# Two transformer blocks on one core: the feed-forwards in two phases, their down products by seven, each down unit passing four banks once per product kind

## The chip, the cores and the metric

The kernel runs on one core of one Trainium2 chip. The metric is the device time in microseconds, the median of several runs. Smaller is better.

## What is computed

Two transformer blocks in a row on a sequence of 1024 tokens of width 1024, in float32. The change touches only their two feed-forwards:

```python
def conv_glu(hn, w_up, conv_f_w, conv_f_b, w_down):          # first block
    up = hn @ w_up
    gate = jax.nn.gelu(causal_dwconv(up[..., :D_FF], conv_f_w, conv_f_b), approximate=False)
    return (gate * up[..., D_FF:]) @ w_down
...
    y = (jax.nn.silu(u @ w_gate[l]) * (u @ w_up[l])) @ w_down[l]   # second block
```

D_FF is 2816 and CONV_F is 3. The result of each is added to the running activations, in the second block after a norm.

## The kernel before

Activations lie transposed, channels on the 128 partitions and tokens along the row. A float32 product is made of three passes: weights and activations are each split into a high and a low part, and high x high, high x low and low x high are summed in PSUM. One matmul has 128x128 weights and 512 columns.

The 2816 hidden channels are 22 tiles, handled as 11 chunks of two tiles (FC = 11). The first chunk's gate and up products are made in the plain way. For each of the other ten, two *pairs* (a gate tile and an up tile each) are made by Strassen's scheme: seven products of 12 matmuls (`part_product`, L1104; four blocks of 128 channels, three passes each) in place of eight. Each product's result goes to a PSUM bank of its own (`pair_banks`), and VectorE combines them (`pair`, L2855), scales them by the norm, applies the convolution in the first feed-forward (`gate_in`), and multiplies gate and up (`hidden`, L2853). Between the pairs of one chunk and those of the next stands the down product of the chunk before (`down_half`, L1157): 8 output tiles x 2 hidden tiles x 2 halves x 3 passes, 96 matmuls, whose results VectorE adds to the running sum in `W` (`add_down`, L2909). The last chunk's down product stands at the end (`last_half`).

The weights come in parts of 128x512 (`part`, over `w_raw`), fetched by SyncE. For each part or sum of parts, ScalarE makes the high part (`high`, L1897) and POOL the low part (`low`, L559) into a ring of three places. POOL also makes the four sums of parts per pair that the scheme needs (L566, L571, L575, L577). VectorE makes the low parts of activations (`diff_lo`, L2798, `act_lo`) and of the hidden tiles (`g_lo`, L2899). Each engine has its own list of instructions in program order; semaphores tie them: `parts_high` and `parts_split` count high and low parts, `product_quarters` products of TensorE, `evacuated` the results that VectorE took away.

Per chunk TensorE has 2 x 84 + 96 = 264 matmuls. The loop over chunks is a hardware loop, whose first and last turn are written out.

```python
for k in range(4):
    w = slice(k * P, (k + 1) * P)
    for i, (a, x) in enumerate(((ring_hi, hi), (ring_hi, lo), (ring_lo, hi))):
        last = pe.matmul(out, a[slot][:, w], x(k), start=(k == 0 and i == 0), stop=(k == 3 and i == 2))
```

## Time and profile before

| | |
|---|---|
| median of 3 runs | 2813.38 us (2813.02 to 2814.61) |
| span of the profiled execution | 2812.4 us |
| TensorE busy | 2756.6 us, 13262 matmuls |
| VectorE busy | 1763.2 us |
| POOL busy | 1365.9 us |
| ScalarE busy | 1027.8 us |
| first feed-forward | about 719 to 1357 us |
| second feed-forward | about 2160 to 2790 us |

Busy time of TensorE is of pipelined matmuls whose durations overlap (one shows 0.389 us), so their pace is read from start to start or from the chain of work that ended last. PE is TensorE, DVE is VectorE, ACT is ScalarE, POOL is GpSimd and SP is SyncE. A line "L559" is a line of the kernel.

### The profile page before, as it was taken

The numbers are of one execution on the slowest core, as the hardware profiler recorded it, in microseconds if no ns is written. First come the engines' busy times: TensorE is split into PE (matmuls) and PEld (weight loads), VectorE is DVE, ScalarE is ACT, GpSimd is POOL, SyncE is SP. The second block draws the span as 40 slices with busy tenths as digits, with TensorE's granted clock in tenths as the row PEclk, the third lists the DMA queues.
The fourth block names the chain that finished last, engine by engine and source line by source line (L and its number), as shares of the span: only waits on it lengthen the run. The fifth ranks groups of instructions, "written<-read, shape, count | busy, mean of one in ns | idle before, by whom it ended". The sixth has DMA issues, their size and how long they took to land.

```text
span 2812.4 us, 36491 instructions
## 1 busy us (share of the span) xinstructions
PE 2756.6 (98%) x13262; PEld 2267.9 (81%) x13262; DVE 1763.2 (63%) x1889; ACT 1027.8 (37%) x1638; POOL 1365.9 (49%) x774
## 2 busy tenths in 40 slices
PE   8999999999999999999999999999999999999999
PEld 6888788888788888888887777778876888888886
DVE  7988552336976667776845446883369656555556
ACT  4256531332422222222413435553456222222224
POOL 4322212214666667666566331543254765566663
PEclk9999999999999999999999999999999999999999
DMA  4101322011111111112322110432023111111113
GB/s 151 38 23 38 105 97 83 31 67 46 46 52 45 52 52 48 63 52 82 128 92 96 46 38 17 140 114 82 23 96 118 49 56 60 48 47 55 51 56 134
DMA packets 72274, 191.31 MB, mean 68 GB/s; under 512 B 7792, under 2 KB 8048, under 8 KB 71408
## 3 DMA queue, kind: packets, MB, share of 16 engines
q1 hardware_dynamic: 61920, 157.12, 16.7%
q10 hardware_dynamic: 10256, 32.86, 3.2%
q8 instruction: 65, 1.06, 0.2%
q14 instruction: 33, 0.27, 0.0%
HBM read 172.65 MB, written 17.30 MB: 68 GB/s over the span
## 4 chain that ended last, share of the span: by engine, by line
PE 57%; issue 23%; POOL 12%; DVE 4%; ACT 2%; DMA 1%; POOLq 0%; ACTq 0%; DVEq 0%; SPq 0%
PE products L651 20%; PE products L1111 8%; PE others L1111 7%; PE others L1157 5%; PE products L1157 5%; POOL w_lo L559 4%; POOL w_lo L502 2%; POOL w_raw L577 1%; POOL w_raw L575 1%; PE others L651 1%; PE products L1047 1%; DVE work L2427 1%; DMA w_raw<-wstream 1%; POOL w_raw L566 1%; POOL part_sum L571 1%
## 5 line engine op out<-in xcount | busy, mean ns | idle before, releaser
L559 POOL TENSOR_TENSOR w_lo<-w_raw,w_hi 128x512 fp32r<-128x512 f32 x328 | 464.5, 1422 | 442.1 <-ACT w_hi L1897 441.1
L1897 ACT ACTIVATE w_hi<-w_raw 128x512 fp32r<-128x512 f32 x328 | 207.1, 633 | 815.9 <-PE products L1111 209.6
L499 POOL TENSOR_TENSOR w_hi<-w_raw,small 128x1024 fp32r<-128x1024 f32 x54 | 111.1, 2058 | 583.9 <-PE products L651 326.4
L651 PE MATMUL products<-act_hi,w_hi 128*128 128x512 f32 x864 | 346.9, 402 | 1.4 <-DVE act_lo L2383 1.3
L651 PE MATMUL products<-act_lo,w_hi 128*128 128x512 f32 x864 | 337.5, 391 | 0.0
L651 PE MATMUL products<-act_hi,w_lo 128*128 128x512 f32 x864 | 337.5, 391 | 0.0
L502 POOL TENSOR_TENSOR w_lo<-w_raw,w_hi 128x1024 fp32r<-128x1024 f32 x94 | 253.0, 2691 | 144.6 <-ACT w_hi L2226 140.4
L651 PEld LDWEIGHTS products<-act_hi,w_hi 128*128 128x128 f32 x864 | 162.9, 189 | 42.0 <-issue 7.3
L651 PEld LDWEIGHTS products<-act_hi,w_lo 128*128 128x128 f32 x864 | 162.7, 188 | 35.0
L651 PEld LDWEIGHTS products<-act_lo,w_hi 128*128 128x128 f32 x864 | 163.2, 189 | 31.4 <-issue 0.2
L745 PE MATMUL products<-act_hi,w_hi 128*128 128x512 f32 x408 | 167.0, 409 | 7.4 <-DVE act_lo L3329 4.7
L1111 PE MATMUL products<-diff_hi,w_hi 128*128 128x512 f32 x400 | 157.8, 395 | 9.6 <-POOL w_lo L559 5.9
L745 PE MATMUL products<-act_lo,w_hi 128*128 128x512 f32 x408 | 159.8, 392 | 0.0
L745 PE MATMUL products<-act_hi,w_lo 128*128 128x512 f32 x408 | 159.7, 391 | 0.0
L1111 PE MATMUL products<-diff_hi,w_lo 128*128 128x512 f32 x400 | 156.4, 391 | 0.0
L1111 PE MATMUL products<-diff_lo,w_hi 128*128 128x512 f32 x400 | 156.3, 391 | 0.0
L1111 PE MATMUL others<-act_hi,w_hi 128*128 128x512 f32 x400 | 155.6, 389 | 0.0
L1111 PE MATMUL others<-act_lo,w_hi 128*128 128x512 f32 x400 | 155.6, 389 | 0.0
L1111 PE MATMUL others<-act_hi,w_lo 128*128 128x512 f32 x400 | 155.6, 389 | 0.0
L2864 DVE TENSOR_TENSOR work<-work,products 128x512 f32<-128x512 f32 x40 | 27.5, 687 | 179.6 <-PE products L1111 175.8
L2909 DVE TENSOR_TENSOR work<-work,others 128x1024 f32<-128x1024 f32 x76 | 92.7, 1220 | 66.8 <-PE others L1157 64.7
L2909 DVE TENSOR_TENSOR work<-work,products 128x1024 f32<-128x1024 f32 x76 | 92.5, 1217 | 61.7 <-PE products L1157 61.7
(555 smaller groups left out, 6928.0 us busy)
## 6 DMA issues: line engine op xcount, KB each, us to landing
w_raw<-wstream SPq DMA_DIRECT2D x155, 512.0 KB, 3.3
w_raw<-wstream SPq DMA_DIRECT2D x248, 256.0 KB, 2.6
work<-xT ACTq DMA_DIRECT2D x16, 512.0 KB, 8.8
parked<-work ACTq DMA_DIRECT2D x8, 512.0 KB, 3.0
work<-parked ACTq DMA_DIRECT2D x8, 512.0 KB, 5.1
parked<-work ACTq DMA_DIRECT2D x2, 2048.0 KB, 8.7
work<-parked SPq DMA_DIRECT2D x8, 512.0 KB, 7.6
out<-work SPq DMA_DIRECT2D x16, 256.0 KB, 2.3
```

The costliest lines, as they stand in the source:

```text
L499: pool.tensor_tensor(w_hi[:, slot, :], w_raw[:, slot, :], zeros, ALU.add)\
L502: pool.tensor_tensor(w_lo[:, slot, :], w_raw[:, slot, :], w_hi[:, slot, :].bitcast(F32), ALU.subtract).then_inc(s("weights_split"), 1)
L559: pool.tensor_tensor(ring_lo[slot], source, ring_hi[slot].bitcast(F32), ALU.subtract).then_inc(s(signal), 1)
L566: pool.tensor_tensor(part[2], part[0], part[2], ALU.subtract).then_inc(s("parts_summed"), 1)
L571: pool.tensor_tensor(part_sum[:, :], part[3], part[2], ALU.subtract).then_inc(s("parts_summed"), 1)
L575: pool.tensor_tensor(part[0], part_sum[:, :], part[0], ALU.add).then_inc(s("parts_summed"), 1)
L651: last = pe.matmul(out[:, c], a[:, ws, w], x[:, k, c], start=(k == 0 and i == 0), stop=(k == KT - 1 and i == 2))
L745: last = pe.matmul(out, a[:, b % 2, w], x[:, k, c], start=(k == 0 and i == 0), stop=(k == KT - 1 and i == 2))
L1111: last = pe.matmul(out, a[slot][:, w], x(k), start=(k == 0 and i == 0), stop=(k == 3 and i == 2))
L1157: last = pe.matmul(out(2 * n + o)[0][:, t], a[slot][:, w], x(k)[:, t], start=(k == 0 and i == 0), stop=(k == 1 and i == 2))
L1897: act.activation(ring_hi[slot], source, ACT.Copy).then_inc(s("parts_high"), 1)
L2909: dve.tensor_tensor(W[:, o, :], W[:, o, :], down_slots[o % 4], ALU.add).then_inc(s("evacuated"), 1)
```

## The change

**Two phases.** The ten chunks' gate and up pairs now follow each other without a down product between them. Each finished hidden tile is stored in DRAM (`parked_hidden`). After the last pair comes the down product of the first ten chunks as a whole, made by Strassen's scheme as well: outputs, hidden channels and tokens are each halved. It is made in two rounds of five chunks (ROUNDS, ROUND). A round has seven steps (kinds 0 to 6 of products), a step five units, one for each chunk, and a unit 12 matmuls: four output tiles, each in a bank of its own, times three passes. 70 units have 840 matmuls where there were 960. The eleventh chunk's down product stays as it was.

**A unit** (`down_unit`) first passes the four banks with high x high, then with high x low after a wait for VectorE's low part, then with low x high after a wait for POOL's. Results of a chain of steps stay in PSUM (four banks for even steps, four for odd), and VectorE adds them to `W` once per step (`step_added`), 128x512 four times.

**The operands of a unit.** Weight tiles and hidden tiles of a round (20 of 512 KB) are loaded into places that the activations, their differences and their low parts leave (`down_upper`, `down_lower`, `hidden_first`, `hidden_second`), in the first round while the last pair still runs. For kinds 1 to 4 POOL makes one sum of weights per unit (`down_sum`) and VectorE one of hidden tiles (`factor_sum`). The high parts are both ScalarE's, the low of the weights is POOL's (`down_low`), that of the hidden tiles VectorE's (`factor_low`). There are four places for each, so that the high part of unit u waits for the end of unit u-4.

**The pairs** are made in another form of the scheme (Winograd's): sums of products are accumulated in PSUM in three banks per pair, and ScalarE copies a bank's intermediate value out three times (`copied`) before the next product goes on in it. VectorE combines four times per pair in place of seven. One of the low parts gets a fourth place. VectorE's operations of scaling and convolution of a pair are done at the start of the next one. The order of the low parts of differences at the start is another: in the second feed-forward those of the third difference come last, and TensorE's third product waits for eight low parts (four before), the fourth and fifth for twelve (eight and twelve).

Core of the diff:

```diff
-        part_sum = place("part_sum", [P, HALF], F32, over="w_hi", offset=HALF)
+        part_sum = place("part_sum", [P, HALF], F32, over="w_lo", offset=HALF)
+        down_hi, down_lo = ring_hi, ring_lo
+        ring_lo = [*ring_lo[0:3], g_hi[:, 0, 0:HALF]]
+        RING = (0, 1, 2, 0, 1, 2, 3)
...
-        part_source = [part[0], part[1], part[2], part_sum[:, :], part[0], part[1], part[3]]
+        part_source = [part[0], part[1], part_sum[:, :], part[0], part[2], part[1], part[3]]
...
+        parked_hidden = nc.dram_tensor("parked_hidden", (2 * BLOCKED, P, T), F32, kind="Internal").ap()
...
+                    sp.wait_ge(s("parts_split"), of.high(c, 7 * j + 6))
+                    fetch(1, at + gate)
+                    if first:
+                        store_hidden(0, 0)
+                    if j:
+                        store_hidden(c, 0)
+                    else:
+                        store_hidden(c + (-1), 1)
+                    sp.wait_ge(s("parts_split"), of.high(c, 7 * j + 7))
+                    fetch(3, at + up)
...
+                for product, first, second in ((2, (0, 1), ()), (3, (2, 3), ()), (4, (4,), (0, 1))):
+                    sp.wait_ge(s("product_quarters"), of.quarters(FC - 1, 8 + product))
+                    for i in first:
+                        down_tiles(i, 0)
+                        hidden_tiles(i, 0, 0)
+                    for i in second:
+                        hidden_tiles(i, 0, 1)
+                sp.wait_ge(s("product_quarters"), of.quarters(FC - 1, 8 + 6))
+                for i in (2, 3, 4):
+                    hidden_tiles(i, 0, 1)
+                down_tiles_lower(0, 0)
...
+                def down_sum(r, s_, i):
+
+                    n = sum_after(r, s_, i)
+                    if s_ == 1:
+                        pool.wait_ge(s("parts_split"), of.down_high(STEP_UNITS * r + i))
+                        k, count = tile_loaded(AT_FFN[name], "second", i, r)
+                        pool.wait_ge(s(f"x_in{k}"), count)
+                        ins = pool.tensor_tensor(a11(i), a11(i), a21(i), ALU.subtract)
+                    elif s_ == 2:
...
+                        ins = pool.tensor_tensor(spare_w(name, i), a22(i), a11(i), ALU.subtract)
+                    elif s_ == 3:
+                        ins = pool.tensor_tensor(a21(i), a21(i), a22(i), ALU.add)
+                    else:
+                        pool.wait_ge(s("parts_split"), of.down_high(STEP_UNITS * r + ROUND + i))
+                        pool.wait_ge(s("parts_summed"), of.down_summed(sum_after(r, 2, i)))
+                        ins = pool.tensor_tensor(a12(i), a12(i), spare_w(name, i), ALU.subtract)
+                    ins.then_inc(s("parts_summed"), 1)
+
+                def down_low(u):
+
+                    source, slot = part[u - UNITS] if u >= UNITS else down_source(name, *unit_of(u)[1:]), down_slot(u)
+                    pool.wait_ge(s("parts_high"), of.down_high(u))
+                    low_, high_ = (down_lo[slot], down_hi[slot]) if u >= UNITS else (by_o(down_lo[slot]), by_o(down_hi[slot]))
+                    pool.tensor_tensor(low_, source, high_.bitcast(F32), ALU.subtract).then_inc(s("parts_split"), 1)
+
+                chunk(1, True)
+                with pool.Fori(2, FC) as c:
+                    chunk(c)
+                for u in range(UNITS + 4):
+                    if u + 1 < UNITS and 1 <= unit_of(u + 1)[1] <= 4:
+                        down_sum(*unit_of(u + 1))
+                    down_low(u)
...
+                def pair(c, j, after_first=False):
+
+                    n = 7 * j
+                    chain_, other, alone = (bank(m) for m in pair_banks[j])
+                    if not after_first:
+                        pe.wait_ge(s("evacuated"), of.evacuated(c, 4 * j - 4))
+                    part_product(c, n + 1, chain_, *lower_half)
+                    if after_first:
+                        pe.wait_ge(s("evacuated"), of.first_evacuated + 2)
+                    part_product(c, n + 2, alone, *lower_second)
+                    pe.wait_ge(s("parts_copied"), of.copied(c, 3 * j + 1))
+                    part_product(c, n + 3, chain_, *difference[1], start=False)
+                    if after_first:
+                        pe.wait_ge(s("evacuated"), of.first_evacuated + 5)
+                    part_product(c, n + 4, other, *difference[0])
+                    pe.wait_ge(s("parts_copied"), of.copied(c, 3 * j + 2))
+                    part_product(c, n + 5, chain_, *third, start=False)
+                    pe.wait_ge(s("parts_copied"), of.copied(c, 3 * j + 3))
+                    part_product(c, n + 6, other, *upper_second, start=False)
+                    pe.wait_ge(s("evacuated"), of.evacuated(c, 4 * j + 2))
+                    part_product(c, n + 7, chain_, *upper_half, start=False, done=2)
+
+                def down_unit(u):
+
+                    r, s_, i = unit_of(u)
+                    g, slot, x = STEPS * r + s_, down_slot(u), u % 4
+                    pe.wait_ge(s("parts_high"), of.down_high(u))
+                    pe.wait_ge(s("factor_hi"), of.factor_high(u))
+                    fresh = s_ in (0, 1, 3) and i == 0
+                    for m, (a, v) in enumerate(((down_hi, factor_hi), (down_hi, factor_lo), (down_lo, factor_hi))):
+                        if m == 1:
+                            pe.wait_ge(s("factor_lo"), of.factor_low(u))
+                        elif m == 2:
+                            pe.wait_ge(s("parts_split"), of.down_high(u))
+                        for o in range(4):
+                            if not i and not m:
+                                pe.wait_ge(s("evacuated"), of.evacuated(BLOCKED, 4 * (g + 1)) if g < 2 else of.added(4 * (g - 2) + o + 1))
+                            w = slice(o * P, (o + 1) * P)
+                            last = pe.matmul(step_bank(g, o), a[slot][:, w], v[x], start=(fresh and m == 0),
+                                             stop=(i == ROUND - 1 and m == 2), skip_group_check=True)
+                    last.then_inc(s("product_quarters"), 1 + (8 * BLOCKED - UNITS if u == UNITS - 1 else 0))
...
+                def copied(c, j, n, times=1):
+
+                    act.wait_ge(s("product_quarters"), of.quarters(c, 8 * j + (1, 3, 4)[n]))
+                    kept = W[:, 16 + j, :]
+                    if n == 0:
+                        act.wait_ge(s("hidden_stored"), of.stored(c + (-1), j))
+                    elif n == 2:
+                        act.wait_ge(s("ff_hidden"), of.hidden(c, j - 1))
+                        if isinstance(c, int) and c == 1:
+                            act.wait_ge(s("factor_lo"), of.factors_low + 16)
+                    to = (kept[:, 0:HALF], kept[:, HALF:T], up_tile(name, j)[:, HALF:T])[n]
+                    source = bank(first_banks[0] if times > 1 else pair_banks[j][(0, 0, 1)[n]])
...
+                def pair(c, j):
+
+                    before = (c, 0) if j else (c + (-1), 1)
+                    scaled(*before)
+                    gate_first(c, j)
+                    hidden(*before)
+                    up_second(c, j)
+                    gate_second(c, j)
+                    up_first(c, j)
...
+                def factor_sum(r, s_, i):
+
+                    n = sum_after(r, s_, i)
+                    if s_ == 1:
+                        dve.wait_ge(s("factor_lo"), of.factor_low(STEP_UNITS * r + i))
...
+                            dve.wait_ge(s("ff_hidden"), of.hidden(BLOCKED, 2))
+                        k, count = tile_loaded(AT_FFN[name], "second", i, r)
+                        dve.wait_ge(s(f"x_in{k}"), count)
+                        dve.wait_ge(s("factor_made"), of.factor_made(sum_after(r, 1, i)))
+                        ins = dve.tensor_tensor(spare_x(name, i), b22(i), b11(i), ALU.subtract)
+                    elif s_ == 3:
+                        ins = dve.tensor_tensor(b12(i), b22(i), b12(i), ALU.subtract)
+                    else:
+                        dve.wait_ge(s("factor_lo"), of.factor_low(STEP_UNITS * r + ROUND + i))
+                        dve.wait_ge(s("factor_made"), of.factor_made(sum_after(r, 2, i)))
+                        ins = dve.tensor_tensor(b21(i), b21(i), spare_x(name, i), ALU.subtract)
+                    ins.then_inc(s("factor_made"), 1)
+
+                def factor_low(u):
+
+                    r, s_, i = unit_of(u)
+                    if u + 1 < UNITS and 1 <= unit_of(u + 1)[1] <= 4:
+                        factor_sum(*unit_of(u + 1))
+                    dve.wait_ge(s("factor_hi"), of.factor_high(u))
+                    dve.tensor_tensor(factor_lo[u % 4], factor_source(name, s_, i), factor_hi[u % 4].bitcast(F32), ALU.subtract)\
+                       .then_inc(s("factor_lo"), 1)
+
+                def step_added(g):
+
+                    r, s_ = g // STEPS, g % STEPS
+                    o0, half = ((0, 0), (0, 0), (0, 1), (4, 1), (4, 1), (0, 1), (4, 0))[s_]
+                    dve.wait_ge(s("product_quarters"), of.unit(ROUND * (g + 1) - 1))
+                    if g:
+                        dve.wait_ge(s("evacuated"), of.added(4 * g))
...
+                    for o in range(4):
+                        to = W[:, o0 + o, half_of(half)]
+                        if not conv_tiles and g in (0, 2, 3, 6):
+                            ins = dve.tensor_copy(to, step_bank(g, o))
+                        else:
+                            ins = dve.tensor_tensor(to, to, step_bank(g, o), ALU.add)
+                        ins.then_inc(s("evacuated"), 1)
```

POOL in the down product of the second and later chunks before: the four low parts of a chunk, one per 24 matmuls (`w_raw` is the fetched part, `w_hi` and `w_lo` the places of the split parts).

```order
L559 TENSOR_TENSOR w_lo_53<-w_raw_51,w_hi_52 128x512 [waits parts_high]
L558 REGISTER_ALU
L559 TENSOR_TENSOR w_lo_53<-w_raw_51,w_hi_52 128x512 [waits parts_high]
```

POOL in the first round's step of kind 2 after the change (`raw` and `work` hold the loaded tiles, L752 is a sum, L766 a low part):

```order
L752 TENSOR_TENSOR work_54<-raw_86 128x512 [waits parts_summed]
L766 TENSOR_TENSOR w_lo_53<-work_54,w_hi_52 128x512 [waits parts_high]
L752 TENSOR_TENSOR work_54<-raw_86,work_54 128x512 [waits parts_summed]
L766 TENSOR_TENSOR w_lo_53<-work_54,w_hi_52 128x512 [waits parts_high]
L752 TENSOR_TENSOR work_54<-raw_86,work_54 128x512 [waits parts_summed]
L766 TENSOR_TENSOR w_lo_53<-work_54,w_hi_52 128x512 [waits parts_high]
```

A low part per 24 matmuls became a sum and a low part per 12.

VectorE in the down product before, of the first feed-forward: additions of results in PSUM (`products`, `others`), and the two low parts of the next hidden tiles once per chunk.

```order
568 L2909 TENSOR_TENSOR work<-work,others 128x1024 [waits product_quarters]
569 L2904 REGISTER_ALU
570 L2909 TENSOR_TENSOR work<-work,others 128x1024 [waits product_quarters]
571 L2904 REGISTER_ALU
572 L2909 TENSOR_TENSOR work<-work,products 128x1024 [waits product_quarters]
573 L2904 REGISTER_ALU
574 L2909 TENSOR_TENSOR work<-work,products 128x1024 [waits product_quarters]
575 L2904 REGISTER_ALU
576 L2909 TENSOR_TENSOR work<-work,others 128x1024 [waits product_quarters]
577 L2896 ISA
578 L2899 TENSOR_TENSOR g_lo<-work,g_hi 128x1024 [waits ff_g_hi] x2
```

VectorE at the start of the down phase's first round after the change (L3160 a sum, L3184 a low part, L3080 the last chunk's product of gate and up, L3201 the addition of a step's banks):

```order
562 L3160 TENSOR_TENSOR raw_86<-raw_86 128x512 [waits factor_lo,dve_chain]
563 L3184 TENSOR_TENSOR act_lo_50<-work_54,act_hi_49 128x512 [waits factor_hi]
564 L3160 TENSOR_TENSOR raw_86<-raw_86 128x512 [waits factor_lo]
565 L3184 TENSOR_TENSOR act_lo_50<-work_54,act_hi_49 128x512 [waits factor_hi]
566 L3160 TENSOR_TENSOR work_54<-work_54 128x512 [waits factor_lo]
567 L3184 TENSOR_TENSOR act_lo_50<-work_54,act_hi_49 128x512 [waits factor_hi]
568 L3080 TENSOR_TENSOR work_54<-work_54 128x1024 [waits ff_gate,evacuated]
569 L3201 TENSOR_TENSOR work_54<-work_54,products 128x512 [waits product_quarters]
570 L3201 TENSOR_TENSOR work_54<-work_54,products 128x512 x3
571 L3160 TENSOR_TENSOR work_54<-work_54 128x512 [waits factor_lo]
572 L3184 TENSOR_TENSOR act_lo_50<-raw_86,act_hi_49 128x512 [waits factor_hi]
```

Between the additions of two steps there now stand five sums and five low parts whose operands all lie in SBUF.

## Rows read from the trace of the kernel before

**Rows 1.** The page: TensorE's busy time, and its granted clock in 40 slices.
```profile
PE 2756.6 (98%) x13262; PEld 2267.9 (81%) x13262; DVE 1763.2 (63%) x1889; ACT 1027.8 (37%) x1638; POOL 1365.9 (49%) x774
...
PEclk9999999999999999999999999999999999999999
```

**Rows 2.** Windows of both feed-forwards: length, busy us, clock, DMA share, GB/s.
```profile
719.00:1357.00 638.00, 632.23 (x2773) 519.07 (x2772) 458.24 (x393) 183.86 (x266) 419.89 (x266) 1.00 0.17 59
...
2168.00:2768.00 600.00, 595.68 (x2619) 492.14 (x2618) 349.31 (x317) 163.61 (x243) 371.76 (x257) 1.00 0.17 59
```

**Rows 3.** Chain that ended last: start, us, what; first, then second feed-forward.
```profile
824.72 5.45 PE others L1111 x24
...
885.22 5.45 PE others L1111 x24
...
2228.07 10.88 PE products L1111 x48
...
2268.88 5.44 PE products L1157 x24
...
2287.91 10.88 PE products L1111 x48
```

**Rows 4.** TensorE's waits in the first feed-forward: us, times, longest.
```profile
PE products L1111 <- POOL w_lo L559: 5.7, 12, 1.4
```

**Rows 5.** Instructions of a line: duration in ns, minimum/median/maximum.
```profile
L559 POOL TENSOR_TENSOR w_lo<-w_raw,w_hi x328: 1284/1297/4038, 719.5 to 2768.7; 128x512 fp32r<-128x512 f32 x164
...
L2798 DVE TENSOR_TENSOR diff_lo<-work,diff_hi x16: 678/685/1780, 700.3 to 2176.1; 128x512 fp32r<-128x512 f32 x16
...
L1897 ACT ACTIVATE w_hi<-w_raw x328: 612/633/637, 718.8 to 2767.3; 128x512 fp32r<-128x512 f32 x164
```

**Rows 6.** Timeline of POOL, then of DVE, 2163 to 2173: start, us, instruction.
```profile
2164.23 1.74 POOL L559 TENSOR_TENSOR w_lo<-w_raw,w_hi 128x512 fp32r<-128x512 f32 x1
2165.93 1.74 POOL L575 TENSOR_TENSOR w_raw<-part_sum,w_raw 128x512 f32<-128x512 f32 x1
2167.63 1.75 POOL L559 TENSOR_TENSOR w_lo<-part_sum,w_hi 128x512 fp32r<-128x512 f32 x1
...
2163.04 3.48 DVE L2809 TENSOR_TENSOR diff_lo<-diff,diff_hi 128x512 fp32r<-128x512 f32 x2
...
2167.05 6.22 DVE L2798 TENSOR_TENSOR diff_lo<-work,diff_hi 128x512 fp32r<-128x512 f32 x4
```

**Rows 7.** Timeline of DVE, 2239 to 2241: operations that follow each other at once.
```profile
2239.82 0.69 DVE L2869 TENSOR_TENSOR work<-work,products 128x512 f32<-128x512 f32 x1
2240.42 0.68 DVE L2873 TENSOR_TENSOR tmp<-work,products 128x512 f32<-128x512 f32 x1
```

**Rows 8.** Timeline of POOL, then of DVE, 2277 to 2280.
```profile
2277.78 1.30 POOL L559 TENSOR_TENSOR w_lo<-w_raw,w_hi 128x512 fp32r<-128x512 f32 x1 [4.14 <-ACT w_hi L1897]
2279.04 1.29 POOL L566 TENSOR_TENSOR w_raw<-w_raw 128x512 f32<-128x512 f32 x1
...
2277.07 1.22 DVE L2909 TENSOR_TENSOR work<-work,others 128x1024 f32<-128x1024 f32 x1 [1.22 <-PE others L1157]
```

**Rows 9.** Timeline, 1171 to 1176: POOL beside a DVE operation of 1024 columns.
```profile
1172.79 2.28 POOL L571 TENSOR_TENSOR part_sum<-w_raw 128x512 f32<-128x512 f32 x1
1175.03 1.30 POOL L559 TENSOR_TENSOR w_lo<-w_raw,w_hi 128x512 fp32r<-128x512 f32 x1
...
1171.64 2.27 DVE L2882 TENSOR_TENSOR tmp<-tmp,rstd 128x1024 f32<-128x1024 f32 x1
```

**Rows 10.** DMA: GB/s in 40 slices of 0 to 60 us; a load's size and landing.
```profile
GB/s 0 152 410 401 421 428 408 410 412 404 412 412 404 16 0 0 0 0 179 309 350 126 10 229 120 0 0 8 295 46 0 0 0 0 0 0 0 0 158 191
...
w_raw<-wstream SPq DMA_DIRECT2D x155, 512.0 KB, 3.3
```

**Rows 11.** Timeline of PE at the start of the second feed-forward.
```profile
2173.32 0.50 PE L1111 MATMUL products<-diff_hi,w_hi 128*128 128x512 f32 x1 [3.70 <-DVE diff_lo L2798]
...
2174.99 0.63 PE L1111 MATMUL products<-diff_hi,w_hi 128*128 128x512 f32 x1
2175.42 0.63 PE L1111 MATMUL products<-diff_lo,w_hi 128*128 128x512 f32 x1
```

686 lines of the change are left out of this document (392 added, 294 removed).

## The prediction, made before the changed kernel was run

> **What bounds the kernel now.** I read the page first: TensorE (PE) is busy 98% of the span at a granted clock in the top tenth [rows 1], and the two stretches that hold the feed-forwards, 638 and 600 us, show 632 and 596 us of PE work at clock 1.00 [rows 2]. Busy time does not say how fast it goes, so next comes the chain that ended last. There 24 matmuls of 512 columns take 5.44 us, 0.2267 us each, and a chunk of the second feed-forward starts 59.84 us after the one before it, which is 264 x 0.2267 = 59.84 [rows 3]. So the second feed-forward waits for nothing in its loop. In the first one a chunk takes 60.50 us [rows 3], 0.66 us more, and the waits of PE name POOL's low parts for it: 5.7 us in 12 waits [rows 4]. The kernel is bound by the number of 512-column matmuls, and only removing some of them, with the others still fed, can shorten it.
>
> **What it removes.** Per chunk the down product falls from 96 matmuls to 7 x 12 = 84. Ten chunks and two feed-forwards: 240 matmuls x 0.2267 = **54.4 us less**. Gate and up products stay at 84 per pair. If nothing else changed, the time would be 2813.4 - 54.4 = 2759.0. All durations below come from one execution whose span is 2812.4; the median of the runs is 1.0 us above it, which is carried through unchanged.
>
> **What it adds.** The down work used to lie in every chunk, with one low part of POOL per 24 matmuls (5.44 us). Now it is a phase of its own, 70 units of 12 matmuls, 2.72 us each. A unit needs a weight part and a hidden part, each split: POOL makes the low of the one, VectorE (DVE) the low of the other, ScalarE both highs (0.63 us each [rows 5], 1.3 of 2.72, so it is covered). Of the 35 units of a round, the 20 of kinds 1 to 4 need one sum more on POOL and one more on DVE. DVE also adds four banks per five units, but those have one operand in PSUM.
>
> Alone, a POOL operation of 128x512 repeats after 1.26 us (2277.78 to 2279.04) and a DVE one after 0.60 (2239.82 to 2240.42) [rows 7, 8]. Two of each are 2.5 and 1.2 us, both inside 2.72. That is the tempting sum. But the rows say these do not run beside each other. From 2163 to 2173 us both engines worked back to back on such operations with both inputs in SBUF: POOL started one each 1.70 us, and DVE took 1.74 and 1.55 us each [rows 6]. So POOL and DVE together get one pair of operations done per 1.70 us. A PSUM add costs POOL nothing: beside L2909 its operation took 1.30 [rows 8]. With 1024 columns on DVE, POOL's takes 2.28 where it has 1.30 else, about 1.0 us more [rows 9].
>
> A unit with sums therefore takes 2 x 1.70 = **3.40 us** of the two engines, against 2.72 of PE; one without takes 1.70. Over a round that is 20 x 3.40 + 15 x 1.70 = 93.5 of 95.2 us: it fits as an average, and only the order decides. Four slots of split parts let POOL run ahead. Its low of unit u can be ready 0.63 + 1.26 = 1.9 us after unit u-4 ends, and PE needs it 3 x 2.72 + 8 x 0.2267 = 10.0 us after that end. The lead is thus at most 8.1 us.
> - Second round: units 35 to 39 and the ten before leave POOL about 1 us spare each, so the lead is full. The 20 dense units fall behind by 20 x 0.68 = 13.6; less 8.1 is 5.5 us of PE waits.
> - First round: there is no lead. The tiles of a down unit come by DMA into the place of operands that the last pair frees product by product. With 410 GB/s [rows 10] a 512 KB tile takes 1.28 us. Sixteen are asked for from 13.6 to 2.7 us before the last pair's end, four at its end. The first four and all behind them queue: from -13.6 + 1.9 us of latency (3.3 to landing less 1.3) 16 tiles end at +8.8, and the 17th, which POOL's first sum (before the low of unit 4) waits for, at +10.1. That sum and low end at +12.6; PE needs the low at 4 x 2.72 + 1.81 = +12.7. Lead zero, so all 13.6 us show. On top lie three DVE operations of 1024 columns in this stretch (the last chunk's hidden product and its two lows), 3 x 1.0; DVE has three of its own operations done before POOL starts, 3 x 0.44 less. Together 15.3.
>
> So 20.8, say 21 us per feed-forward, **42 us more** in both. The bounds: nothing if DVE's operations fell beside POOL's (2.5 < 2.72), and, if no overlap at all is left, 2 x (1.26 + 0.60) = 3.72 us a unit, hence 2 x 20 x 1.00 - 8.1 + 1.7 = 33.6 each, 67 us. I take 3.40, since that row has just these operations.
>
> The Trainium skill, "SBUF — State Buffer", section "Who interferes with whom", says that a VectorE instruction with two SBUF inputs and a GpSimd one that reads SBUF share one read port, held for the whole instruction while the other blocks fully. By that rule a pair of operations would take the sum of both, 1.86 us, and the total would be 2829 us; by the row it is 1.70, and the total 2804.
>
> **The pairs.** Two new things. (1) Each product's bank is copied or combined on the way, since sums are now accumulated in PSUM: three copies on ScalarE (0.63 us, as its other operations of this size [rows 5]) between products of 2.72 us; each has one whole product to be done in, so nothing. (2) The pairs follow each other each 19.04 us, without the 21.8 us of down work that let POOL catch up. POOL has 11 operations, 11 x 1.26 = 13.9; DVE's two-SBUF operations beside them take in the first feed-forward (scale, three of the convolution, half a scale, the hidden product) 4 x 1.0 + 2 x 0.45 = 4.9 more: 18.8 of 19.04. It fits by a hair. From POOL's last low of a pair, which cannot start before 4 x 2.72 + 1.2 = 12.1, to the low of the next pair's product 4 there are 9 operations (11.3 us) and three or four collisions (3.5 to 4.5): ready at 26.9 to 27.9, needed at 27.2. A wait of 0 to 0.8 us a pair, 20 pairs, against 0.33 now. I take it to stay at 0.33, **0 change**, with -7 and +9 us as its ends. In the second feed-forward there is no convolution: 2.4 us of collisions, 16.3 of 19.04, nothing.
>
> **The queues.** Per feed-forward SyncE gets 20 stores of hidden tiles (512 KB) and 20 loads of them; the weights' bytes stay the same, now 20 loads of 512 KB. DMA is busy 0.17 of its time in these stretches [rows 2], so some 20 MB more over 600 us cost nothing as bandwidth. In a pair the store waits for the hidden product, and behind it is queued the load of part 3, which POOL's second sum needs; but that load waits in any case for POOL's seventh low (14 us into the pair), which comes after the hidden product (13 us). Nothing, and up to the 0.8 us a pair above if the hidden product is late.
>
> **The start of the second feed-forward.** PE now waits 3.70 us for DVE's lows L2798 before the fourth product, until 8 of them are made, and the rows show them ending at 2173.3 (the fifth product goes once 12 are made) [rows 11]. After the change the third product waits for the 8, the fourth for the 12: one product later, **2.7 us more**. In the first feed-forward the lows end before PE comes to them.
>
> **Sum.** 2813.4 - 54.4 + 42 + 0 + 2.7 = 2803.7, say **2804 us**. Between this and no gain stands little: with p for the pace of a dense unit, each feed-forward loses 40 (p - 2.72) - 6.4, and the gain is gone at p = 3.53 us.
>
> **Rivals.**
> - *The two engines keep up.* DVE works only two thirds of a unit, and in the gaps POOL runs at 1.26; ScalarE lies between a sum and its low, which spreads them. With p = 3.0, the second round is covered, the first loses 5.6 + 1.7: 2 x 7.3 = 15, and 2776 us; with p under 2.72, 2762. For it: POOL had 1.29 in about half of all cases of L559 (median 1297 ns [rows 5]). Against it: those are the cases in which DVE had nothing of this kind to do, which is not so here. Chance 0.20.
> - *Slower: no overlap is left.* p = 3.72, because a blocked operation waits for the whole of the other and starts late again behind ScalarE's high; then 2813.4 - 54.4 + 67 + 2.7 = 2829 us. It decides from p = 3.53. For it: L559's maximum of 4038 ns and 1780 for L2798 [rows 5]: an operation can be passed over. Against it: 10 us of rows 6 at 1.70. Chance 0.22. The rule of the Trainium skill cited above ("SBUF — State Buffer", "Who interferes with whom") would give this time too.
> - *Slower: the pairs.* At 0.8 us a pair in the first feed-forward and p = 3.40: 2804 + 9, and with late DMA (3 us more in each first round) 2819. Chance 0.10.
> - *The clock falls.* PE waits 0.7 us in each dense unit and changes the bank with each matmul. After one wait of 3.70 us matmuls went at 0.43 instead of 0.227 us for a few [rows 11], the 1.2 GHz level. Were 80 dense units to run at it, 80 x (5.1 - 3.4) = 136 us more. No wait expected is near 3.7, so 0.04. The Trainium skill, "TensorE: Matmul & The Clock Gate", section "A second HAM failure mode: psum-queue depth-cycling", tells of a kernel whose clock swung as it cycled through PSUM banks. The trace has bank changes each third matmul at full pace [rows 3], none at each.
> - My forecast, p from 3.25 to 3.5, 2791 to 2811 us, the only case that fits the row made of the same operations: 0.44.
>
> **How the numbers follow.** A measurement tells about 0.2%, 5.6 us, from no change. Of the forecast's 0.44, 0.28 lie under 2807.8 and 0.16 above; with the first rival, faster is 0.48. Same: 0.16 and a tenth from the edges of the slower rivals (whose smaller sizes lie there), 0.24 with rounding. Slower: 0.28. The range reaches from 2776 (half of the first rival left out) to 2836 (the clock and the worst of no overlap left out).
>
> **What would show it.** In the changed profile: matmuls 13262 less 240; pace 0.227 kept in the pairs (19.04 us a pair); in the down phases PE's waits put down to POOL's low part of the units (or DVE's), some 15 us in a first round and 5 in a second; units of 3.4 us in kinds 1 to 4 and 2.72 in kinds 0, 5 and 6; POOL's operations there at 1.70 from start to start. I would be wrong if dense units show 2.72 or over 3.5, if PE waits for weights' tiles beyond unit 5, or if the clock's row drops.

## The result, and the profile after

The changed kernel takes 2831.4 us (median of 4 runs, 2830.3 to 2835.1), the kernel before 2813.2 us (4 runs, 2812.5 to 2814.6) on the same chip: a ratio of 1.0064, 95% interval 1.0050 to 1.0078. It is 18 us slower where 9 us faster was forecast, and inside the range. The rows below are of one execution whose span is 2828.4 us (2812.4 before).

The page has 13022 matmuls, 240 less than [rows 1], and the clock's row looks as before; POOL's busy time rose from 1365.9 to 1591.4 us:

```profile
PE 2726.5 (96%) x13022; PEld 2224.0 (79%) x13022; DVE 1785.3 (63%) x1909; ACT 1131.9 (40%) x1874; POOL 1591.4 (56%) x914
...
PEclk9999999999999999999999999999999999999999
```

So TensorE is 30 us less busy and the span is 16 us longer. The places where one kind of matmul takes over from another in TensorE's timeline give the balance. The first matmul of the pairs starts at 727.77 us before and 728.38 after (+0.6). From there to the end of the first feed-forward it is 629.96 us before and 634.76 after (+4.8), then to the second one's pairs 803.4 and 802.3 (-1.2), from there to its half products at the end 605.34 and 616.77 (+11.4), and the rest is +0.3. Each feed-forward lost 120 matmuls, 27.2 us. The down phase, from its first matmul to that of the eleventh chunk, should be 840 x 0.2267 = 190.4 us. It is 1116.31 to 1341.38 and 2556.71 to 2782.16, so 225.1 and 225.5 us: 34.7 and 35.1 us too long, **70 us in both, where 42 were forecast**. What is left is -2.6 us in the first feed-forward and +3.6 in the second.

Windows of both down phases (length, then busy us of PE, PEld, DVE, ACT, POOL with the number of instructions, granted clock, DMA share, GB/s), to be held against [rows 2]:

```profile
1117.00:1341.00 224.00, 202.96 (x837) 156.79 (x836) 192.59 (x170) 83.50 (x144) 177.78 (x112) 0.98 0.22 79
2557.00:2782.00 225.00, 203.12 (x840) 156.93 (x839) 189.18 (x167) 83.90 (x144) 177.72 (x112) 0.98 0.22 79
```

VectorE (DVE), not POOL, is the busiest engine beside TensorE there. TensorE's waits (us in total, times, longest) say the same, first phase and second:

```profile
PE products L1372 <- DVE act_lo L3184: 11.3, 14, 4.5
PE others L1372 <- DVE act_lo L3184: 6.9, 11, 1.7
PE products L1372 <- POOL w_lo L766: 2.4, 1, 2.4
...
PE products L1372 <- DVE act_lo L3184: 10.6, 13, 4.6
PE others L1372 <- DVE act_lo L3184: 6.9, 11, 1.6
PE products L1372 <- POOL w_lo L766: 3.9, 1, 3.9
```

L3184 is VectorE's low part of a hidden tile, L766 POOL's of a weight tile. POOL holds TensorE up once in a phase, at its start. The waits add up to 20.6 and 21.4 us; most of the rest of the 34.7 and 35.1 stands in the busy time above, 203.0 and 203.1 us for 190.4, since a matmul before a wait isn't overlapped by the next (it counts 0.39 us and not 0.2267) and some ran at a lower clock.

**One dense kind.** VectorE's timeline (start us, us) from the four adds of one kind (L3201) to those of the next, in kinds 1 to 4 of the first round:

```profile
1159.74 2.47 DVE L3201 TENSOR_TENSOR work<-work,others 128x512 f32<-128x512 f32 x4
1162.13 0.68 DVE L3169 TENSOR_TENSOR w_raw<-raw,work 128x512 f32<-128x512 f32 x1
1162.73 1.77 DVE L3184 TENSOR_TENSOR act_lo<-work,act_hi 128x512 fp32r<-128x512 f32 x1
1164.42 1.78 DVE L3169 TENSOR_TENSOR w_raw<-raw,work 128x512 f32<-128x512 f32 x1
...
1176.32 1.78 DVE L3184 TENSOR_TENSOR act_lo<-raw,act_hi 128x512 fp32r<-128x512 f32 x1
1178.03 2.47 DVE L3201 TENSOR_TENSOR work<-work,products 128x512 f32<-128x512 f32 x4
```

It never stands idle. Five sums (L3169, L3171) and five lows (L3184), one operation at 0.60 us and nine at 1.70 from start to start, and 2.4 for the adds: 1178.03 - 1159.74 = 18.29 us for five units, **3.66 us a unit** against 2.72 of TensorE. Each 1.70 is the pace of [rows 6]: it lies beside an operation of POOL.

**Kind by kind.** TensorE's rows change from "products" to "others" and back with each kind, so its timeline gives what each kind of five units took, in us (13.60 is TensorE's own pace; first feed-forward, here and in all kernels below unless it says otherwise):

| kernel | round 1, kinds 0 to 4 | round 2, kinds 1 to 4 |
|---|---|---|
| after | 17.68, 16.86, 22.46, 18.26, 15.83 | 15.82, 15.84, 17.45, 16.87 |
| e1_narrow_adds | 18.40, 16.67, 19.46, 17.03, 16.32 | 14.52, 17.04, 16.97, 16.33 |
| e2_sums_on_vector | 16.67, 18.23, 17.27, 17.16, 20.30 | 13.60, 14.17, 17.17, 20.25 |
| e3_dense_on_vector | 17.00, 14.72, 16.86, 15.08, 14.78 | 13.60, 13.60, 14.27, 14.77 |
| e4_early_tiles | 20.05, 19.15, 16.97, 17.43, 16.90 | 15.79, 15.85, 17.41, 16.92 |
| e4, second feed-forward | 14.42, 19.40, 19.95, 17.44, 16.90 | 15.81, 15.88, 17.39, 16.89 |
| e5_last_lows_late | 18.47, 16.25, 18.04, 18.27, 17.58 | 15.82, 15.83, 17.44, 16.91 |
| e9_narrow_weight_sums | 16.45, 15.92, 22.04, 13.60, 13.60 | 13.84, 14.32, 13.99, 13.60 |
| e11, second feed-forward | 13.60, 13.61, 13.60, 13.60, 13.59 | 13.60, 13.59, 13.62, 14.41 |

All other kinds stand at 13.60 in each of them. In the changed kernel the first round is 23.1 us over (15.3 forecast), the second 11.6 (5.5 forecast); in its second feed-forward they are 23.5 and 11.6.

### The profile page after: what moved, and what is told of

Its sections match the earlier page's. It is cut to its first block, busy times and chain, and to the rows that moved or that the text cites. A ratio compares the mean times of both kernels' runs of the same rounds, so it can differ in the third digit from the quotient of the medians.

```text
span 2828.4 us, 36043 instructions
## 1 busy us (share of the span) xinstructions
PE 2726.5 (96%) x13022; PEld 2224.0 (79%) x13022; DVE 1785.3 (63%) x1909; ACT 1131.9 (40%) x1874; POOL 1591.4 (56%) x914
## 4 chain that ended last, share of the span: by engine, by line
PE 64%; DVE 15%; issue 13%; POOL 3%; DMA 2%; ACT 2%; ACTq 0%; POOLq 0%; DVEq 0%; SPq 0%
PE products L842 20%; PE others L1303 13%; PE products L1303 12%; DVE act_lo L3184 4%; PE products L1372 2%; PE others L1372 2%; POOL w_lo L655 2%; PE products L936 1%; DVE work L3201 1%; PE others L842 1%; DMA w_raw<-wstream 1%; PE products L1238 1%; DVE work L2654 1%; DMA raw<-wstream 1%; PE products L965 1%
## 5 line engine op out<-in xcount | busy, mean ns | idle before, releaser
L652 POOL TENSOR_TENSOR w_hi<-w_raw,small 128x1024 fp32r<-128x1024 f32 x54 | 111.0, 2055 | 585.0 <-PE products L842 326.9
L842 PE MATMUL products<-act_hi,w_hi 128*128 128x512 f32 x864 | 346.6, 401 | 1.5 <-DVE act_lo L2610 1.3
L711 POOL TENSOR_TENSOR w_lo<-w_raw,w_hi 128x512 fp32r<-128x512 f32 x200 | 307.3, 1541 | 67.9 <-ACT w_hi L2101 67.9
L842 PE MATMUL products<-act_lo,w_hi 128*128 128x512 f32 x864 | 337.5, 391 | 0.0
L842 PEld LDWEIGHTS products<-act_hi,w_hi 128*128 128x128 f32 x864 | 162.9, 189 | 42.1 <-issue 7.3
L2101 ACT ACTIVATE w_hi<-w_raw 128x512 fp32r<-128x512 f32 x240 | 146.2, 626 | 123.4 <-PE others L1303 51.3
L936 PE MATMUL products<-act_hi,w_hi 128*128 128x512 f32 x408 | 165.9, 407 | 8.5 <-DVE act_lo L3634 4.9
L936 PE MATMUL products<-act_lo,w_hi 128*128 128x512 f32 x408 | 159.0, 390 | 0.0
L766 POOL TENSOR_TENSOR w_lo<-raw,w_hi 128x512 fp32r<-128x512 f32 x72 | 111.6, 1550 | 51.9 <-ACT w_hi L2149 51.9
L1303 PE MATMUL others<-act_hi,w_hi 128*128 128x512 f32 x336 | 131.6, 392 | 3.8 <-DVE tmp L3096 3.8
L1303 PE MATMUL others<-act_lo,w_hi 128*128 128x512 f32 x336 | 131.3, 391 | 0.0
L1303 PE MATMUL products<-act_hi,w_hi 128*128 128x512 f32 x304 | 118.4, 389 | 0.0
L1303 PE MATMUL products<-act_lo,w_hi 128*128 128x512 f32 x304 | 118.3, 389 | 0.0
L785 POOL TENSOR_TENSOR w_hi<-w_raw,small 128x1024 fp32r<-128x1024 f32 x22 | 46.7, 2124 | 120.7 <-PE products L842 104.8
L766 POOL TENSOR_TENSOR w_lo<-work,w_hi 128x512 fp32r<-128x512 f32 x58 | 90.6, 1567 | 23.8 <-ACT w_hi L2149 23.8
L936 PEld LDWEIGHTS products<-act_hi,w_hi 128*128 128x128 f32 x408 | 76.6, 188 | 32.5 <-DVE act_lo L3634 8.2
L1372 PE MATMUL products<-act_lo,w_hi 128*128 128x512 f32 x280 | 80.1, 408 | 22.2 <-DVE act_lo L3184 21.9
```

The costliest lines, as they stand in the source:

```text
L652: pool.tensor_tensor(w_hi[:, slot, :], w_raw[:, slot, :], zeros, ALU.add)\
L711: pool.tensor_tensor(ring_lo[slot], part_source[(n - 1) % 7], ring_hi[slot].bitcast(F32), ALU.subtract)\
L766: pool.tensor_tensor(low_, source, high_.bitcast(F32), ALU.subtract).then_inc(s("parts_split"), 1)
L785: pool.tensor_tensor(high, w_raw[:, b % 2, :], zeros, ALU.add).then_inc(s("weights_high"), 1)
L842: last = pe.matmul(out[:, c], a[:, ws, w], x[:, k, c], start=(k == 0 and i == 0), stop=(k == KT - 1 and i == 2))
L936: last = pe.matmul(out, a[:, b % 2, w], x[:, k, c], start=(k == 0 and i == 0), stop=(k == KT - 1 and i == 2))
```

## The experiments

Where a comparison with the changed kernel is made, its time on that chip is taken as 1.0064 of the kernel before's. The down phases are measured in each kernel's own trace, as above; the changed kernel's are 225.1 and 225.5 us, 450.5 together.

| run | us, median | ratio to before, 95% | against the changed kernel, us | down phases, us |
|---|---|---|---|---|
| e1_narrow_adds | 2824.9 | 1.0028 (1.0018 to 1.0038) | -9 | 220.7, 221.4 |
| e2_sums_on_vector | 2822.2 | 1.0021 (1.0011 to 1.0030) | -12 | 222.8, 219.5 |
| e3_dense_on_vector | 2786.5 | 0.9898 (0.9881 to 0.9914) | -47 | 202.7, 202.9 |
| e4_early_tiles | 2826.1 | 1.0040 (1.0026 to 1.0054) | -8 | 224.5, 222.1 |
| e5_last_lows_late | 2826.5 | 1.0048 (1.0032 to 1.0065) | -6 | 222.6, 222.5 |
| e6_one_wait_a_unit | 2837.6 | 1.0088 (1.0070 to 1.0106) | +5 | 228.6, 228.4 |
| e7_start_waits | 2832.0 | 1.0064 (1.0047 to 1.0081) | -1 | 225.3, 225.9 |
| e8_all_four | 2778.9 | 0.9875 (0.9859 to 0.9892) | -54 | 200.6, 197.2 |
| e9_narrow_weight_sums | 2790.8 | 0.9914 (0.9897 to 0.9931) | -43 | 205.4, 205.5 |
| e10_adds_later | 2832.5 | 1.0059 (1.0042 to 1.0076) | -1 | 225.3, 225.1 |
| e11_vector_and_scalar | 2774.6 | 0.9853 (0.9836 to 0.9869) | -59 | 198.6, 191.2 |

The intervals are about 0.15% each way, 4 us, so for small differences the down phases tell more than the medians.

**VectorE's adds (e1).**

```diff
+                        n = 64 if g % STEPS in (0, 1, 2, 3) else HALF
-                            ins = dve.tensor_tensor(to, to, step_bank(g, o), ALU.add)
+                            ins = dve.tensor_tensor(to[:, 0:n], to[:, 0:n], step_bank(g, o)[:, 0:n], ALU.add)
```

> The changed kernel (2831.4 us), but VectorE's four adds of a product kind's banks into the hidden tiles are 64 columns wide instead of 256 for the four kinds that end in a dense stretch (it leaves out three quarters of those sums). Theory A, VectorE is the bound of the dense kinds: a dense kind of five units takes 18.3 us there, ten operations at 1.70 and 2.47 us of adds less what they save; without most of the adds it is ten operations at 1.70 = 17.0 us, 3.40 a unit. Of the 32 kinds of both feed-forwards 16 are dense and each add stands in one: 16 x about 1.2 = 19 us less, 2812 (2806 to 2817). Theory B, the prediction's: VectorE's adds lie beside GpSimd's work and cost nothing, the port alone sets 3.40: no change, 2831 (2827 to 2833), and what is beyond 3.40 comes from the late tiles.

(The adds are 512 columns wide, not 256 as it says there; seven eighths of those sums are left out, and the copies that stand for some of them in the second feed-forward are narrowed in the same way.) Measured: down phases 4.3 and 4.1 us shorter, 8.4 together. That is less than half of the 19 us of theory A and not the nothing of theory B. VectorE's timeline, again from adds to adds:

```profile
1163.37 0.60 DVE L3202 TENSOR_TENSOR work<-work,others 128x64 f32<-128x64 f32 x4
...
1178.65 1.78 DVE L3184 TENSOR_TENSOR act_lo<-raw,act_hi 128x512 fp32r<-128x512 f32 x1
1180.35 0.60 DVE L3202 TENSOR_TENSOR work<-work,products 128x64 f32<-128x64 f32 x4
```

16.98 us a kind in the first round instead of 18.29, as theory A has it. But over the four dense kinds the first round gains 3.9 us, of which kind 0 gives 0.7 back, and the second round only 1.1 (66.0 to 64.9). In the changed kernel's second round TensorE takes 16.5 us a kind on average, not 18.3. VectorE goes from adds to adds in 18.3, 15.0 and 18.3 us there (they start at 1250.44, 1268.74, 1283.74 and 1302.00). In the short one POOL, which gets ahead beside adds (1.30 us there, as in [rows 8]), runs out of high parts and stands idle for 1.9 us, in which VectorE gets four operations at 0.60. VectorE, then POOL, in the changed kernel:

```profile
1271.13 0.68 DVE L3169 TENSOR_TENSOR w_raw<-raw,work 128x512 f32<-128x512 f32 x1
...
1272.94 0.68 DVE L3184 TENSOR_TENSOR act_lo<-w_raw,act_hi 128x512 fp32r<-128x512 f32 x1
1273.54 1.78 DVE L3171 TENSOR_TENSOR raw<-work,raw 128x512 f32<-128x512 f32 x1
...
1273.13 1.64 POOL L766 TENSOR_TENSOR w_lo<-work,w_hi 128x512 fp32r<-128x512 f32 x1 [1.91 <-ACT w_hi L2149]
```

So 3.66 us a unit holds while POOL is never idle. Narrow adds save 1.3 us a kind (18.29 less 16.98), 5.2 in four: about three quarters of it show in the first round and a fifth in the second.

**Who does the sums (e2, e3, e9).** These move or thin POOL's work.

```diff
e2: down_sum by VectorE, behind factor_low(u), before unit u + 1
-                        down_sum(*unit_of(u + 1))          (pool)
+                        down_sum(*unit_of(u + 1))          (dve)
e3: the same, and for kinds 1 to 4 also
+                    if 1 <= unit_of(u)[1] <= 4:
+                        down_low(u)                        (dve)
e9: down_sum stays POOL's, in kinds 1, 3 and 4 with 64 of 512 columns
+                    n = lambda v: v[:, :, :, 0:16]
```

> The changed kernel, but the weight sums of the down products (80 of 256 x 128 elements a partition in all, one before each dense unit) are done by VectorE instead of GpSimd. Theory A, a GpSimd operation costs VectorE 1.10 us (1.70 against 0.60) and VectorE is the bound: a dense kind takes VectorE 15 x 0.60 + 5 x 1.10 + 2.47 = 17.0 us instead of 18.3, so 16 x 1.3 = 21 us less, 2810 (2803 to 2820). Theory B, VectorE has its own work as limit and takes five operations more at the 1.70 that they take beside GpSimd: 15 x 1.70 = 25.5 us a kind, 16 x 7.2 = 115 us slower, 2946. Theory C, the late tiles are what costs: no change.

> The changed kernel, but in the dense kinds both the weight sums and the low parts of the weights go to VectorE, and GpSimd does nothing there. Theory A: a dense kind takes VectorE 20 x 0.60 + 2.47 = 14.5 us, 2.9 a unit instead of 3.66, against 2.72 of TensorE: 16 x 3.8 = 61 us less, at most what the down phases lie over 190.4 us each (70 us), 2770 (2763 to 2780). Theory B, VectorE's operations are that long for a reason of their own (1.70 each): 20 x 1.70 = 34 us a kind, 250 us slower. Theory C, TensorE's change of bank at every matmul or its clock holds the units over 2.72: the time falls to no less than 2800.

> The changed kernel, but GpSimd's sums of weights for kinds 1, 3 and 4 are 64 columns instead of 512 (most of those sums is left out); for kind 2 they stay whole. So in one run kind 2 has VectorE beside two full operations of GpSimd a unit and kinds 1, 3 and 4 beside one. VectorE's own work is the same in all. Theory A, each full operation of GpSimd lengthens one of VectorE's from 0.60 to 1.70 us and VectorE is the bound: kinds 1, 3 and 4 take it 5 x 1.70 + 5 x 0.60 + 2.47 = 14.0 us, so units of 2.8 us, while kind 2 stays at 17 to 18.3 less the lead: some 3 us less for each of 12 kinds, 36 to 45 us in all, 2790 (2782 to 2800). Theory B, VectorE is slow by its own instructions: no change. Theory C, TensorE's changes of bank or its clock set the units: no change in kinds 1, 3 and 4.

e3 settles the main question. VectorE does twenty operations a kind instead of ten, and the phases fall by 22.5 us each. Its timeline, from adds to adds, and two of the rows between:

```profile
1153.22 2.47 DVE L3213 TENSOR_TENSOR work<-work,others 128x512 f32<-128x512 f32 x4
...
1162.56 0.68 DVE L3197 TENSOR_TENSOR w_lo<-work,w_hi 128x512 fp32r<-128x512 f32 x1
1163.16 0.69 DVE L3152 TENSOR_TENSOR raw<-work,raw 128x512 f32<-128x512 f32 x1
...
1168.32 1.87 DVE L3213 TENSOR_TENSOR work<-work,products 128x512 f32<-128x512 f32 x3
```

15.1 us a kind against 18.3: the operations are at 0.60 now. Ten of POOL's went, which had cost VectorE 9 x 1.10 = 9.9 us, and cost it 10 x 0.60 = 6.0 when done by itself: 18.3 - 9.9 + 6.0 = 14.4, and 0.15 us a unit on top in which it waits for ScalarE's high. The gain was 47 us where 61 was expected: the 61 took each of the sixteen dense kinds to stand at 18.3 us, but those of the second rounds stood at 16.5. A second round gave 9.7 us, a first one 12.7 and 12.9. Kinds 1 and 2 of the second round are at 13.60 now: the change of bank at every matmul, which they have like all others, costs nothing, which rules theory C out. e2 gained less than half of its 21 us in the down phases, and has a wait of its own: the sum of unit u + 1 stands behind the low of unit u, which stands behind both of ScalarE's highs, which wait for the sum of unit u. ScalarE's timeline shows this ring, 3.25 us a turn:

```profile
1168.03 0.63 ACT L2126 ACTIVATE w_hi<-raw 128x512 fp32r<-128x512 f32 x1 [2.09 <-DVE raw L3179]
...
1171.28 0.63 ACT L2126 ACTIVATE w_hi<-raw 128x512 fp32r<-128x512 f32 x1 [2.10 <-DVE raw L3179]
```

Four such turns and one of 4.19 us (1174.53 to 1178.72), in which the adds stand, make 17.19 us. The 17.16 of kind 3 lies near theory A's 17.0, but is this sum and not that one. Kind 4 takes 20.3 us in both rounds, more than in the changed kernel, with waits of 2.1 and 2.2 us for VectorE's low part in the first; why it does was not followed up.

e9 shows the same with VectorE's own work untouched. In one trace, VectorE in kind 2 (whole sums on POOL), then in kind 3 (narrow ones):

```profile
1142.96 1.77 DVE L3169 TENSOR_TENSOR work<-work,raw 128x512 f32<-128x512 f32 x1
1144.65 1.78 DVE L3184 TENSOR_TENSOR act_lo<-raw,act_hi 128x512 fp32r<-128x512 f32 x1
...
1162.35 1.77 DVE L3171 TENSOR_TENSOR raw<-work,raw 128x512 f32<-128x512 f32 x1
1164.04 0.81 DVE L3184 TENSOR_TENSOR act_lo<-w_raw,act_hi 128x512 fp32r<-128x512 f32 x1
1164.77 1.78 DVE L3171 TENSOR_TENSOR raw<-work,raw 128x512 f32<-128x512 f32 x1
```

Beside POOL's whole operations a pair of its operations takes 3.4 us, beside one whole and one narrow 2.42 (1162.35 to 1164.77). Kinds 3 and 4 stand at 13.60 at once, kind 2 stays slow, and the time is 2790.8 where 2790 was expected (43 us less than the changed kernel on that chip, for 36 to 45).

**The tiles (e4).**

```diff
-TILES_OF = [2, 2, 2, 2, 2, 4, 2, 4]
+TILES_OF = [2, 2, 2, 4, 2, 2, 2, 4]
...
-                for i in (2, 3, 4):
-                    hidden_tiles(i, 0, 1)
                 down_tiles_lower(0, 0)
+                hidden_tiles(2, 0, 1)
                 sp.wait_ge(s("product_quarters"), of.quarters(FC - 1, 16))
-                for i in range(1, ROUND):
-                    down_tiles_lower(i, 0)
+                down_tiles_lower(1, 0)
+                down_tiles_lower(2, 0)
+                for i in (3, 4):
+                    hidden_tiles(i, 0, 1)
+                    down_tiles_lower(i, 0)
```

> The changed kernel, but the tile that the first dense unit needs is the 13th in the queue and not the 17th (its own semaphore, its transfer right behind the sixth product of the last pair), the others in the order of their use. Theory A: the first dense unit of each feed-forward starts on the tile; it was there 13.0 us after the down phase began, is now some 6 us earlier, and the whole dense stretch moves: 4 to 6 us less a feed-forward, 2821 (2818 to 2825). Theory B, the rate of VectorE alone sets the end of the stretch and the start is hidden: 2831.

The first lines of the edit (with `TILE_SEM`, not shown) are part of it: in the changed kernel the tiles of the first and the second dense unit count on one semaphore, so the first unit, whose own tile is the 16th, waits for the 17th too. By the trace they landed at 1127.89 and 1129.55, so 1.7 us of the wait come from the shared semaphore.

In the changed kernel the chain that ended last passes through the 17th tile, asked for at 1116.51; then the same chain goes on over VectorE:

```profile
1097.43 19.04 PE others L1303 x84
1116.51 13.04 DMA raw<-wstream
1129.63 0.64 ACT act_hi L2163
1130.29 1.22 DVE act_lo L3184
```

In e4 POOL's first sum starts 4.5 us earlier (1125.20 instead of 1129.68). The second feed-forward gains 3.4 us by it, the first only 0.6. There VectorE has the convolution of the last hidden tile to do in this stretch (SCALAR_TENSOR_TENSOR, 1.28 us each in the changed kernel), and what POOL starts earlier lies beside it. VectorE, POOL and TensorE in e4:

```profile
1125.07 1.28 DVE L3052 SCALAR_TENSOR_TENSOR work<-work,cols 128x1023 f32<-128x1023 f32 x1
1126.39 2.19 DVE L3053 SCALAR_TENSOR_TENSOR work<-work,cols 128x1022 f32<-128x1022 f32 x1
1128.51 1.76 DVE L3145 TENSOR_TENSOR work<-work,rstd 128x512 f32<-128x512 f32 x1
...
1125.20 2.30 POOL L748 TENSOR_TENSOR raw<-raw 128x512 f32<-128x512 f32 x1 [2.70 <-DMA raw<-wstream]
...
1133.67 2.07 PE L1374 MATMUL products<-act_lo,w_hi 128*128 128x512 f32 x4 [4.83 <-DVE act_lo L3186]
```

The wait for POOL (2.42 us at 1132.70 in the changed kernel) has become one of 4.83 us for VectorE. Theory A comes close for the second feed-forward (3.4 us for 4 to 6), B holds for the first.

**The last lows (e5).**

```diff
-LAST_HIGH, LAST_LOW = 8, 10
+LAST_HIGH, LAST_LOW = 28, 30
```

> The changed kernel, but the two 1024-column lows of the last hidden tiles (VectorE, 4.54 us beside GpSimd) and their highs stand behind unit 28 and 30, in a kind without sums, instead of behind unit 8 and 10 at the start of the dense stretch. Theory A, VectorE is the bound there: each microsecond taken out of the dense stretch comes back, 4.5 us in ffn1 and as much in ffn2, less what the clock does: down phases 9 us shorter in all, 2823 on the chip of the first comparison. Theory B, GpSimd or the port as a sum is the bound and this is hidden: no change.

Theory A, with 2.5 and 3.0 us less a phase instead of 4.5: kind 2 falls from 22.46 to 18.04, and 1.75 of it come back in kind 4, in which POOL now stands idle for 1.8 us instead of 3.2. This also shows where the clock falls. In the changed kernel the two lows make the longest wait of the phase, and the matmuls behind it run slowly; TensorE, then windows of that stretch (clock is the number ahead of the last two), in the changed kernel and in e5:

```profile
1154.25 1.07 PE L1372 MATMUL products<-act_hi,w_hi 128*128 128x512 f32 x4
1159.87 2.07 PE L1372 MATMUL products<-act_lo,w_hi 128*128 128x512 f32 x4 [4.54 <-DVE act_lo L3184]
1161.74 1.91 PE L1372 MATMUL products<-act_hi,w_lo 128*128 128x512 f32 x4
...
1159.00:1165.00 6.00, 5.13 (x14) 4.06 (x15) 6.00 (x8) 1.78 (x3) 6.00 (x5) 0.57 0.01 3
```

```profile
1159.00:1165.00 6.00, 4.21 (x18) 2.85 (x17) 6.00 (x5) 2.27 (x4) 6.00 (x4) 1.00 0.00 0
```

Behind the wait of 4.54 us four matmuls take 1.7 to 1.9 us instead of 0.91, which is the 1.2 GHz level; the granted clock is 0.57 over those 6 us. Without that wait it is 1.00. It falls once more in the changed phase, behind the 2.42 us at 1132.70 (0.57 from 1133 to 1137). VectorE works on without a gap meanwhile, so most of the loss lies under its bound; e5's gain isn't split between the two.

**The second half of the change (e6).**

```diff
-                    for m, (a, v) in enumerate(...):
-                        if m == 1:
-                            pe.wait_ge(s("factor_lo"), of.factor_low(u))
-                        elif m == 2:
-                            pe.wait_ge(s("parts_split"), of.down_high(u))
-                        for o in range(4):
+                    pe.wait_ge(s("factor_lo"), of.factor_low(u))
+                    pe.wait_ge(s("parts_split"), of.down_high(u))
+                    for o in range(4):
+                        for m, (a, v) in enumerate(...):
```

> The changed kernel, but each down unit waits for all its four operands ahead of its first matmul, and then makes each bank's three products in a row (as the kernel before did), instead of once through the four banks for each product kind with the waits between. It tests the second half of the change by itself. Theory A, VectorE's rate sets the dense kinds whatever TensorE does while it waits: the down phases grow by no more than one or two us for each of the two rounds, where the lead runs out, 4 us in all and at most 8; the sparse kinds stay at 13.60 us for five units. Theory B, the waits between are what keeps TensorE fed: 0.9 us of each of 80 dense units are lost, 72 us slower.

6.4 us more in the two phases, theory A. The kinds without sums stay at 13.60. So passing the banks once per kind of product with waits between is worth about 6 us here, and only where TensorE's lead ends: kind 0 of the first round goes from 17.68 to 21.11, the first dense kind of the second round from 15.82 to 17.37. In the saturated kinds (18.26 and 18.13) it makes no difference.

**The start of the second feed-forward (e7).**

```diff
-                    pe.wait_ge(s("factor_lo"), factors + 8)
+                    pe.wait_ge(s("factor_lo"), factors + (4 if name == "ffn2" else 8))
-                    pe.wait_ge(s("factor_lo"), factors + (12 if name == "ffn2" else 8))
+                    pe.wait_ge(s("factor_lo"), factors + 8)
```

> The changed kernel, but the third product of ffn2's first pair waits for the four lows of its own difference alone and the fourth product for the next four, as VectorE makes them in that order in ffn2. Theory A: TensorE waited 6.60 us there for the last low of both; it needs the fourth only, whose end is four times 0.68 us earlier: 2.7 us less, in ffn2's first pair alone. Theory B, VectorE's later work is late anyway and the wait moves on to the next product: no change.

TensorE's waits from 2160 to 2200, in the changed kernel (the row of before is in [rows 11]) and in e7:

```profile
PE products L1303 <- DVE diff_lo L3025: 6.6, 1, 6.6
PE others L1303 <- DVE tmp L3096: 1.5, 1, 1.5
```

```profile
PE products L1303 <- DVE diff_lo L3025: 5.2, 2, 3.7
```

8.1 us of waits have become 5.2, which is theory A's 2.7 in this place. The medians don't show it (-1, with 4 either way). In the traces, the second feed-forward's pairs up to its down phase take 391.3 us in the changed kernel and 391.3 to 392.2 in all others without this edit. With it they take 389.5 in e7 and 389.6 in e8, about 2 us less, but 392.4 in e11, where TensorE waits at four places (2.2, 1.2, 2.7 and 1.2 us). So its worth for the whole is not settled.

**VectorE's lead (e10).**

```diff
-                    if u % ROUND == 2:
+                    if u % ROUND == 4 and u > 4:
                         step_added(u // ROUND - 1)
```

> The changed kernel, but VectorE makes a kind's four adds two units later (ahead of the low part of the fifth unit of the next kind instead of the third). With the adds ahead of the third unit VectorE stands idle 2.89 us for the end of the kind while two lows of the next are ready (at 1234.80), and its lead at the second dense stretch is 2.1 us. Theory A, that order costs the lead: two to three us more of it, 2 us less in each feed-forward, 4 in all, 2827. Theory B, the lead is set by the four places of the operands alone: no change.

No change of the time, theory B. But the lead did grow: the wait at 1234.80 is gone, and kind 1 of the second round takes 14.17 us instead of 15.82. Kinds 2 and 3 then take 18.27 and 18.28 instead of 15.84 and 17.45, since POOL no longer stands idle in them, and the four together take 65.6 us instead of 66.0. What the larger lead gained was lost again with POOL's idle time. The changed kernel's rows show why the lead is small there, VectorE then TensorE:

```profile
1240.23 1.78 DVE L3160 TENSOR_TENSOR raw<-raw 128x512 f32<-128x512 f32 x1
...
1245.34 1.78 DVE L3184 TENSOR_TENSOR act_lo<-work,act_hi 128x512 fp32r<-128x512 f32 x1
...
1249.11 1.07 PE L1372 MATMUL products<-act_lo,w_hi 128*128 128x512 f32 x4
```

The low of unit 40 is done at 1247.05 and needed at 1249.11, 2.1 us ahead. Its high had come by 1241.4, so that low alone would have been 7.1 us ahead. VectorE makes two sums and the low of unit 39 first, each at 1.70 beside POOL, since the dense work begins with the sum for unit 40 while unit 39's low is still to be made.

**Together (e8, e11).** e8 is e3, e4, e5 and e7 in one. e11 adds

```diff
+                        if u % STEP_UNITS >= ROUND:
+                            down_sum(*unit_of(u + 1))      (ahead of the low of unit u)
...
+                    act.activation(W[:, o0 + o, half_of(half)], step_bank(g, o), ACT.Copy).then_inc(s("evacuated"), 1)
```

the second in the second feed-forward for steps 0, 2, 3 and 6, whose banks are only copied there, one bank beside each of four units on ScalarE.

> Dense kinds on VectorE alone (sums and low parts of the weights), the early tiles, the last lows late and the start's waits together. The dense kinds on VectorE alone left the down phases at 202.7 and 202.9 us, 12.3 above TensorE's 190.4; dense kinds took 15.4 us there, 14.5 of VectorE's work. Theory A, VectorE's rate still sets them: the last lows take 1.2 to 2.4 us out of each dense stretch, the tiles 2 us, so each phase takes about 199 us, and with 2.7 us at the start the time is some 10 us below the 2786.5 of that kernel, 2776. Theory B, what is left comes from TensorE (its clock behind each stall): the same 2786.

> The kernel with all four edits (dense kinds on VectorE alone, early tiles, late last lows, the start's waits; 2778.9), and two more: each weight sum goes ahead of the low part of the unit before, so that ScalarE isn't kept waiting (0.16 us a unit), and in ffn2 ScalarE copies the banks of steps 0, 2, 3 and 6 out, one beside each of four units, in VectorE's place. Theory A, VectorE's rate is still the bound (15.1 us a dense kind): ffn2 loses 2.4 us in three of four dense kinds and reaches TensorE's 13.6 in them, its down phase falls from 197.2 to 192, ffn1's by about 2 of its 200.6; together 7 us less, 2772 (2768 to 2776). Theory B, ScalarE's copies delay its highs and the wait moves there: no gain in ffn2.

e8 reached 2778.9 (2776 expected), e11 **2774.6 us, 1.47% below the kernel before** (1.31% to 1.64%). In e11 the second feed-forward's down phase is 191.2 us against TensorE's 190.4; its row of windows, inside the phase:

```profile
2535.00:2725.00 190.00, 189.48 (x836) 156.51 (x835) 156.67 (x231) 91.03 (x160) 44.38 (x32) 1.00 0.27 92
```

The first feed-forward's still has 8 us to give, and its adds are all true adds, so none could be made a copy.

## Why the prediction was wrong

- **The matmuls** went as told: 240 fewer, 19.04 us a pair but for the first three pairs of the first feed-forward and the first two of the second (20.35 to 27.75 us), and 13.60 us for five units wherever operands are there.
- **The step that failed: the 42 us of the down phases, which were 70, were worked out from a joint pace of both engines ("A unit with sums therefore takes 2 x 1.70") and from POOL's lead, where VectorE alone was the bound.** Two terms were wrong by it, the pace and the lead. That VectorE's operations take 1.70 us beside POOL's, the mechanism of the forecast, came true (e3, e9).
- **The pace: "A PSUM add costs POOL nothing" was taken as costing nothing at all.** VectorE has the adds on top of what it shares with POOL. While both are saturated it takes 9 x 1.70 + 0.60 + 2.4 = 18.3 us a kind, 3.66 a unit, past the 3.53 that the prediction itself named as break-even. Over all dense kinds of a feed-forward TensorE's average is 3.48 us a unit, with VectorE's lead and POOL's idle time in it. e1, without most of the adds, has phases shorter by 4.3 and 4.1 us.
- **The lead was mis-sized.** The prediction gave the second round 8.1 us, for POOL; VectorE's was 2.1. Sums and lows of the units before are queued ahead of its low at 1.70 each. This is the largest term, 6 us a feed-forward. With p = 3.40 the prediction's formula gives 13.6 - 2.1 = 11.5, and 11.6 was measured, but that p fits here is in part luck: what the adds cost VectorE in this round, POOL's idle time gave back (e1, e10).
- **The first round**, 23.1 and 23.5 for 15.3: the tile landed 13.2 us into the phase (1116.51 + 13.04 less 1116.31) instead of 10.1, worth up to 3.4 (e4), though in the first feed-forward VectorE's convolution stands right behind it; the adds 3.2 and 3.0, net of kind 0; the two last lows cost 4.5 as they stand (e5: 2.5 to 3.0 come back) where 2.0 was put down. These overlap, so they don't add up to the difference by themselves, and its split stays open.
- **The pairs** were taken as unchanged. From the fourth pair on TensorE waits for nothing, where the chunks before took 0.66 us more each ([rows 3], [rows 4]). The first feed-forward gained 2.6 us by it, net of longer first pairs (a new wait of 2.3 us for VectorE in the second one). The rival in which the pairs fall short is out. Why POOL keeps up there better than counted was not tried.
- **The start of the second feed-forward**: 2.7 us forecast for the third product's wait, 2.9 measured (6.60 for 3.70), and a wait of 1.5 us in the second pair that was not foreseen. The whole start is 3.6 us longer. The kernel before has one trace and the wait was 6.6 to 7.8 us in the kernels that start like the changed one, so the 2.9 is uncertain by about 1 us.
- **The rivals.** "No overlap is left" named 2829 us, near the 2831 measured, but its mechanism did not occur: pairs of operations of both engines take 1.70 us, not 1.86, and what a saturated unit took over 3.40 came from the adds. The Trainium skill, "SBUF — State Buffer", section "Who interferes with whom", calls the shared port pair an exclusive lock. Here the trace disagrees in size (1.70 us for a pair of operations that take 1.26 + 0.60 alone) but agrees that operations with one input in SBUF don't contend: VectorE's adds from PSUM stay at 0.60 beside POOL. "The clock falls" occurred twice a phase, at waits of 2.4 and 4.5 us in the first and 3.9 and 4.6 in the second, where the prediction expected none near 3.7. It was priced as if it came with the changes of bank ("TensorE: Matmul & The Clock Gate", "A second HAM failure mode: psum-queue depth-cycling", in the Trainium skill); e9's kinds at 13.60 with a new bank at each matmul show that it did not.

## What to carry to other kernels

Count each engine's work per unit by itself, with the operations that cannot collide too, and take as pace the engine with the most; a joint pace of two engines that share something is a lower bound. Before work is given to POOL, compare what it frees on VectorE (0.60 us here) with what it costs there (1.10 us, where it falls beside an operation with two SBUF inputs): where VectorE is the bound, taking it back is a gain. A lead is what remains when everything queued ahead at the contended pace is taken off, not the room that the buffers give.

## What the runs showed of the hardware

- A 128x512 operation of VectorE with both inputs in SBUF goes from 0.60 to 1.70 us beside one of POOL, which itself goes from 1.26 to 1.70: 20 such operations on VectorE alone, with its four adds, take 15.1 us where ten on each engine took 18.3.
- SCALAR_TENSOR_TENSOR of 1022 columns with both inputs in SBUF collides as well: 1.28 to 2.19 us (e4).
- TensorE passed to another bank at each of 60 matmuls of a kind at its full pace of 0.2267 us (13.60 us a kind; e3, e9, e11).
- In the changed kernel the granted clock fell at every single wait of TensorE of 2.3 us or more in the feed-forwards (2.32, 2.42, 3.94, 4.54, 4.55 and 6.60 us) and at none of the seven of 1.5 to 1.7 us. Between these the runs show no sharp limit: it fell at one of 1.91 us in e3 and not at one of 2.87 us in e2.
